# Outer products of key and value for eight decode samples: 8-row matmuls on TensorE, or ScalarE scaling value rows that a broadcast DMA has spread over the partitions

## The chip, the cores and the metric

One core of one Trainium2 chip runs the whole kernel as one launch. The metric is device time in microseconds (us). The kernel before takes 1415.7 us (median of 3 runs, 1415.12 to 1415.8). Engines go by the names of the profile: PE is TensorE (PEld its weight loads), ACT is ScalarE, DVE is VectorE, POOL is GpSimd, SP is SyncE. POOL and SP issue the DMAs; SPq is SP as the profile lists its DMA issues.

## The reference, cut to what matters

One step of a one-layer decoder: latent attention (MLA) and gated linear attention (GLA) are merged, then come cross attention over 256 memory tokens and a mixture of 32 experts (top 4). It runs for a prompt of 256 tokens and for 8 samples of one token each, all in float32. The change touches the recurrence of the samples alone. Each of the 8 samples has, for each of 4 heads, a state of 128 x 256 numbers:

```python
def gla_sample(q, k, v, la, state):
    def step(st, inp):
        qt, kt, vt, lat = inp
        st = jnp.exp(lat)[..., None] * st + kt[..., :, None] * vt[..., None, :]
        return st, jnp.einsum('bhd,bhdv->bhv', qt, st)
```

For sample b and head h the second term is the outer product of a key of 128 numbers and a value of 256. The new states are an output (512 KB per sample), and the query times the new state goes on into the layer.

## The kernel before, in words

Every engine has its own hand-written program; semaphores S("name") order them. Activations lie transposed, features on the partitions and the 264 tokens (256 of the prompt, 8 samples) along the row. Weights come in 2 MB pieces through ring slots of 16 KB per partition; SP issues them in the order of RING, each when the last reader of its slot is done (L439 to L445). Products go in a fixed order LIN through PSUM banks 0 to 3: `open_bank` waits until the product four places before it has been copied out. Transposes go in a fixed order TURN through banks 5 and 6. A transpose at an even place of TURN is copied out by DVE, at an odd place by ACT (`turn_out`), so taking one name out of TURN swaps the two engines for all names behind it: those of the GLA output (gt0 to gt3, L1012), the memory keys (xk, L1025), the cross attention (xp, xst) and the routing weights (cwt, L1246).

The stage around the change comes after the eight units of prompt attention (L900 to L917), from 218 to 257 us of the span:

- In unit 5, PE transposes the samples' keys (ks, L837), and DVE copies them out, 8 rows to a token. `k_rows` (L1975) are 8 copies of these rows in slot 3, in the copy of sample b all rows but row b set to zero. In unit 7, PE transposes the values: v0 to v3 of the prompt, then v4 and v5 of the samples (L838 to L844), the latter into `vs_tok`, 8 rows to a token.
- `outer_products(b)` on PE (L922): four matmuls with 8 rows of contraction, `k_rows` of b times `vs_tok`, give the four 128 x 256 outer products in banks 5 and 6. It waits until DVE is done with the products of sample b - 1 (state_new), and raises kv_sample.
- DVE (L2002 to L2010) waits for the old state of sample b (state_in) and for kv_sample, makes the new state in place with four `scalar_tensor_tensor`, and raises state_new.
- `state_times_q(b)` on PE (L933) multiplies the query by the new state and raises state_read.
- PE's loop (L952 to L960) is, for b = 0 to 7: outer_products(b); then product gg{b} of the output gate (b < 6) or the prompt's chunk scores A0, A1; then state_times_q(b - 1). After the loop comes state_times_q(7).
- ACT copies gg0 to gg5 out with Silu (L1524), waits for the eighth state_read (L1526), squares the samples' output, copies A0 and A1 out and turns out ko0 (L1527 to L1532). PE multiplies the prompt's keys and values next (L967 to L979).
- POOL (L592 to L602) has all state DMAs in one program. There are four state buffers in SBUF. For b = 0 to 7 it issues the load of state b; for b >= 4 it first waits until the store of state b - 4 has landed and until PE has read that state (L596, L597). For b >= 3 it then issues the store of state b - 3 (`store_state`, L551, which waits for state_new). At b = 2 it waits for the product uv7.
- SP loads the next use of slot 3 (weights zm0) when kv_sample is 8 (L441).

```python
            for b in range(8):
...
                if b >= 4:
                    pool.wait_ge(S(f"state_out{b % 4}"), 16)
                    pool.wait_ge(S("state_read"), b - 3)
                pool.dma_start(st_buf[b % 4], state_gla[0, b].rearrange("h k v -> k h v")).then_inc(S(f"state_in{b % 4}"), 16)
                if b >= 3:
                    store_state(b - 3)
```

Behind this stage stand the rest of GLA, the gates, the output products and the cross attention (to about 490 us), and then the experts, whose 384 MB of weights SP streams from about 418 us on (L475 to L494) as slots come free.

## Time and profile before

| | us |
|---|---|
| median of 3 runs (lowest, highest) | 1415.7 (1415.12, 1415.8) |
| the profiled execution's own time | 1419.78 |
| span of the profiled execution | 1418.0 |
| PE busy of the span | 1338.1 (94%) |
| DVE, ACT, POOL busy | 353.4, 252.4, 84.9 |
| granted TensorE clock, mean of the span | 0.992 |

The span is the stretch that the trace covers; the execution's own time has 1.8 us more around it. The profiled execution is 4.1 us longer than the median of the runs without a profile, so differences are made inside the trace and then put on the median. Busy time of an engine is not the same as work on the path that sets the end. The chain of waits follows that path back from the last instruction. A row of a timeline gives start, duration, engine, line, operation, output and inputs, and in brackets how long the engine had been idle before it and what ended that. Granted clock 1.00 is 2.4 GHz, 0.50 is 1.2 GHz.

### The profile page before, as it was taken

What the parts mean: (1) busy time and instruction counts of PE and PEld (TensorE: products, weight loads), DVE (VectorE), ACT (ScalarE), POOL (GpSimd) and SP (SyncE); (2) the same over time, 40 slices, a digit from 0 to 9 for tenths busy, and PEclk for the clock granted to TensorE, in tenths of its full rate; (3) what the DMA queues carried; (4) which work ended last, traced back from release to release, by engine and by line L of the source; (5) the groups of instructions that cost most, each with busy time, mean ns of one, the idle gap of its engine ahead of it and who ended that gap; (6) DMA issues with size and microseconds to landing.
All of it is one profiled execution on the core that took longest, in us unless ns stands there. A gap on an engine that the chain in (4) does not pass through costs nothing.

```text
span 1418.0 us, 17786 instructions
## 1 busy us (share of the span) xinstructions
PE 1338.1 (94%) x7300; PEld 710.4 (50%) x7300; DVE 353.4 (25%) x775; ACT 252.4 (18%) x543; POOL 84.9 (6%) x104
## 2 busy tenths in 40 slices
PE   7998999899999999999989989899999998998987
PEld 5746887588888734434433424334344243342433
DVE  2753343310134522212212202122022021220112
ACT  3323332421123501101101101011011010110102
POOL 1541211100101000000000000000000000000000
PEclk9999999999999999999999999999999999999999
DMA  9773555923647799999999999999999999999995
GB/s 332 240 262 125 193 181 161 326 98 140 247 169 273 285 428 427 428 428 429 429 428 428 429 428 428 429 428 428 420 429 429 429 428 428 429 428 427 429 427 224
DMA packets 62437, 494.75 MB, mean 349 GB/s; under 512 B 5247, under 2 KB 6472, under 8 KB 37816
## 3 DMA queue, kind: packets, MB, share of 16 engines
q1 hardware_dynamic: 50904, 453.95, 77.1%
q0 software_dynamic: 11488, 40.17, 8.4%
q8 instruction: 32, 0.52, 0.1%
q14 instruction: 13, 0.11, 0.0%
HBM read 487.05 MB, written 7.05 MB: 348 GB/s over the span
## 4 chain that ended last, share of the span: by engine, by line
PE 75%; DMA 20%; DVE 2%; issue 1%; ACT 0%; SPq 0%; POOL 0%; DVEq 0%
PE bank L1183 21%; PE bank L680 16%; PE bank L1210 13%; DMA ring<-in_w_gate_up 11%; DMA arena<-in_w_down 8%; PE bank L1222 4%; PE bank L1169 4%; PE bank L639 3%; PE bank L652 2%; PE bank L790 1%; PE bank L1190 1%; PE bank L704 1%; PE bank L1196 1%; PE bank L1119 1%; PE bank L1033 1%
## 5 line engine op out<-in xcount | busy, mean ns | idle before, releaser
L1183 PE MATMUL bank<-ring,arena 128*64 128x512 f32 x1536 | 344.9, 597 | 7.3 <-DMA ring<-in_w_gate_up 7.3
L1210 PE MATMUL bank<-arena 128*64 128x512 f32 x976 | 225.1, 613 | 32.0 <-DMA arena<-in_w_down 32.0
L1183 PEld LDWEIGHTS bank<-ring,arena 128*64 128x64 f32 x1536 | 104.1, 137 | 224.7 <-issue 205.9
L680 PE MATMUL bank<-arena,ring 128*128 128x264 f32 x896 | 204.9, 388 | 0.0
L680 PEld LDWEIGHTS bank<-arena,ring 128*128 128x128 f32 x896 | 168.2, 190 | 31.9 <-issue 3.9
L1210 PEld LDWEIGHTS bank<-arena 128*64 128x64 f32 x976 | 69.1, 140 | 174.1 <-issue 127.3
L2220 DVE TENSOR_TENSOR resid<-resid,bank 128x264 f32<-128x264 f32 x128 | 55.0, 429 | 375.5 <-PE bank L1222 374.0
L1183 PE MATMUL bank<-arena 128*64 128x512 f32 x512 | 115.5, 593 | 3.9 <-DMA arena<-in_w_gate_up 3.9
L2225 DVE TENSOR_SCALAR arena<-bank 128x512 f32<-128x512 f32 x32 | 22.0, 688 | 323.3 <-PE bank L1183 323.3
L1672 ACT COPY arena<-bank 64x512 f32<-64x512 f32 x63 | 36.5, 580 | 240.3 <-PE bank L1210 239.5
L1183 PEld LDWEIGHTS bank<-arena 128*64 128x64 f32 x512 | 36.3, 137 | 78.5 <-issue 66.8
L1351 ACT ACTIVATE arena<-bank 128x264 f32<-128x264 f32 (+6 forms) x120 | 46.8, 402 | 158.2 <-PE bank L680 117.0
L1664 ACT ACTIVATE arena<-arena 128x512 f32<-128x512 f32 x32 | 20.2, 630 | 306.0 <-DVE arena L2225 306.0
L1222 PE MATMUL bank<-arena 128*128 128x264 f32 x256 | 63.9, 392 | 0.0
L1660 ACT COPY arena<-bank 128x512 f32<-128x512 f32 x32 | 18.8, 587 | 243.5 <-PE bank L1196 243.4
L1169 PEld LDWEIGHTS bank<-arena 128*128 128x128 f32 x512 | 59.6, 192 | 1.0
L1169 PE MATMUL bank<-arena 128*128 128x128 f32 x512 | 60.0, 275 | 0.0
L1222 PEld LDWEIGHTS bank<-arena 128*128 128x128 f32 x256 | 45.9, 189 | 19.6 <-issue 13.0
L680 PE MATMUL bank<-ring 128*128 128x264 f32 (+1 forms) x192 | 44.4, 385 | 1.6 <-DVE ring L2061 1.4
L680 PEld LDWEIGHTS bank<-ring 128*128 128x128 f32 x192 | 35.7, 190 | 7.8 <-DVE ring L2061 1.8
L560 POOL DMA_INDIRECT ring<-in_cache_kv_latent,arena x32 | 33.6, 1050 | 95.9 <-PE bank L890 38.3
L1190 PE MATMUL bank<-arena 32*64 32x512 f32 x256 | 34.8, 612 | 1.5 <-DVE arena L2226 1.5
(317 smaller groups left out, 974.4 us busy)
## 6 DMA issues: line engine op xcount, KB each, us to landing
ring<-in_w_gate_up SPq DMA_DIRECT2D x96, 2048.0 KB, 29.6
arena<-in_w_down SPq DMA_DIRECT2D x61, 2048.0 KB, 22.7
arena<-in_w_gate_up SPq DMA_DIRECT2D x32, 2048.0 KB, 29.2
ring<-in_w_in SPq DMA_DIRECT2D x10, 2048.0 KB, 9.6
ring<-in_w_down SPq DMA_DIRECT2D x3, 2048.0 KB, 44.1
out<-arena POOLq DMA_DIRECT2D x10, 512.0 KB, 5.3
arena<-in_state_gla POOLq DMA_DIRECT2D x8, 512.0 KB, 4.8
ring<-in_w_o_mla SPq DMA_DIRECT2D x2, 2048.0 KB, 8.6
```

The source lines that it names most:

```text
L560: pool.indirect_dma_start(lat[j].rearrange("p a b -> p (a b)"), None, lat_rows, off).then_inc(S(f"lat{j}"), 16)
L639: mm = nc.tensor.matmul(lin_bank(name)[0:m, 0:width], l, r, start=(j == 0), stop=(j == len(parts) - 1))
L652: mm = nc.tensor.transpose(turn_bank(name)[0:m, at:at + k], src, ident[r:r + k, r:r + k])
L680: mm = nc.tensor.matmul(lin_bank(name)[0:m, 0:width], w(ring_name, nk, cols)[:, k, a:a + m], rhs[:, k, 0:width], start=(k == 0), stop=(k = ...
L1169: mm = nc.tensor.matmul(B[2 + 3 * half][:, P * k:P * k + P], hn_tok[:, tt, a:a + P], sel[:, tt, :], start=(tt == 0), stop=(tt == 1))
L1183: mm = nc.tensor.matmul(B[i // 2][CAP * (i % 2):CAP * (i % 2) + CAP, :], xg[:, k, CAP * e:CAP * e + CAP], slot(n)[:, a:a + 512], start=Fal ...
L1190: nc.tensor.matmul(B[q // 2][CAP * (q % 2):CAP * (q % 2) + CAP, :], pick_b[32 * q:32 * q + 32, e, :], b_gu[32 * q:32 * q + 32, :], start=T ...
L1210: mm = nc.tensor.matmul(B[4][CAP * half:CAP * half + CAP, :], hT[:, c, CAP * (k // 4):CAP * (k // 4) + CAP], slot(j)[:, a:a + 512], start= ...
L1222: nc.tensor.matmul(B[5 + c % 3][:, 0:T], y_rows[:, 128 * c:128 * c + 128], wselT, start=True, stop=True)\
L1351: nc.scalar.activation(dst, lin_bank(name)[0:m, 0:width] if src is None else src, func, **kw).then_inc(S("product_out"), 1)
L1672: nc.scalar.copy(y_rows[CAP * odd:CAP * odd + CAP, 512 * half:512 * half + 512], B[4][CAP * half:CAP * half + CAP, :])\
L2220: V.tensor_tensor(h_T[:, c, :], h_T[:, c, :], B[5 + c % 3][:, 0:T], ALU.add).then_inc(S("added"), 1)
```

## The change

PE makes no outer product any more, and the keys of the samples are not transposed (ks is gone from TURN). In unit 7, v4 and v5 are transposed ahead of v0 to v3. POOL writes the samples' value rows to a DRAM tensor `v_rows` (two DMAs of 16 KB), waits for them, and reads each sample's row of 4 KB back to all 128 partitions, 512 KB into one of four buffers `v_wide` in slot 3 (`widen_values`). The first two of these stand before its wait for uv7; for b = 2 to 7 one stands between the load of state b and the store of state b - 3, from b = 4 on behind a wait for kv_sample. They count on the semaphores lat0 to lat3. ACT then makes the outer product: four `activation(Copy)` of 128 x 256 from `v_wide` into banks 5 and 6, each scaled per partition by the key. ACT's order is gg0, outer 0, gg1, outer 1 to gg5, outer 5, outer 6, outer 7. PE's loop is gg0 to gg5, A0, A1, with state_times_q(b - 2) behind step b, and 6 and 7 after the loop. DVE loses the mask and the `k_rows`. ACT's copy of cwt is moved behind its first `gathered`. As ks is gone, DVE and ACT swap the transposes behind it.

```diff
@@ -112,7 +112,7 @@
 AT_UNIT = {1: ["pv0"], 2: ["pv1"], 3: ["ol0", "pv2"], 5: ["pv3"], 6: ["ol1"], 7: [f"uv{h}" for h in range(7)]}
 
 
-TURN_AT_UNIT = {1: ["P1_0", "P1_1"], 2: ["P1_2", "P1_3"], 5: ["ks"], 7: [f"v{n}" for n in range(6)]}
+TURN_AT_UNIT = {1: ["P1_0", "P1_1"], 2: ["P1_2", "P1_3"], 7: [f"v{n}" for n in (4, 5, 0, 1, 2, 3)]}
 
 
 LIN = (["cq0", "cq1", "ckv", "kr", "rotk", "mk0"]
@@ -329,15 +329,15 @@
         v_tok = xview(0, 2048, D)
         ko_tok = xview(2048, 1024, 512)
         AT = xview(3072, 512).rearrange("p (c h t) -> p c h t", c=2, h=H_GLA)
-        vs_tok, ks_tok, row_mask = view(A_SMALL + 256, 512), A[0:64, 14816:15072], view(15072, 32)
-        k_rows = slot(3)[0:64, 0:2048].rearrange("p (b n) -> p b n", b=SAMPLE)
+        vs_tok = view(A_SMALL + 256, 512)
+
+        v_wide = [slot(3)[:, 1024 * i:1024 * i + 1024] for i in range(4)]
+        v_rows = nc.dram_tensor("v_rows", (SAMPLE, H_GLA * DV), F32, kind="Internal").ap()
 
         def row_parts(name):
             if name[0] == "P":
                 c = int(name[3])
                 return [(past[:, 1, 512 * c:512 * c + 512], P, (0, 512))]
-            if name == "ks":
-                return [(ks_tok[32 * g:32 * g + SAMPLE, :], SAMPLE, (256 * g, 256 * g + 256)) for g in range(2)]
             n = int(name[1])
             c, g = n // 2, n % 2
             if n < 4:
@@ -589,13 +589,27 @@
                     pool.dma_start(o_memv_p[0, 0].rearrange("(t p) h d -> p t (h d)", p=P), memv).then_inc(S("stored"), 16)
 
             pool.wait_ge(S("gla_qk"), 1)
+            def widen_values(b):
+                if b >= 4:
+                    pool.wait_ge(S("kv_sample"), b - 3)
+                pool.dma_start(v_wide[b % 4], v_rows[b:b + 1, :].to_broadcast([P, H_GLA * DV])).then_inc(S(f"lat{b % 4}"), 16)
+
             for b in range(8):
                 if b == 2:
+                    turned(pool, "v4")
+                    turned(pool, "v5")
+                    for g in range(2):
+                        pool.dma_start(v_rows[:, 512 * g:512 * g + 512], vs_tok[32 * g:32 * g + SAMPLE, :]).then_inc(S("v_rows"), 16)
+                    pool.wait_ge(S("v_rows"), 32)
+                    widen_values(0)
+                    widen_values(1)
                     lin_full(pool, "uv7")
                 if b >= 4:
                     pool.wait_ge(S(f"state_out{b % 4}"), 16)
                     pool.wait_ge(S("state_read"), b - 3)
                 pool.dma_start(st_buf[b % 4], state_gla[0, b].rearrange("h k v -> k h v")).then_inc(S(f"state_in{b % 4}"), 16)
+                if b >= 2:
+                    widen_values(b)
                 if b >= 3:
                     store_state(b - 3)
             for b in range(5, 8):
@@ -832,16 +846,13 @@
                     pe.wait_ge(S("past_exp"), 2)
                     for c in (2 * u - 2, 2 * u - 1):
                         turn(f"P1_{c}", [(128 * t, past[:, 1, 512 * c + 128 * t:512 * c + 128 * t + 128]) for t in range(4)])
-                if u == 5:
-                    lin_done(pe, "gk3")
-                    turn("ks", [(128 * h, gkT[:, h, PROMPT:T]) for h in range(H_GLA)])
                 if u == 7:
                     lin_done(pe, "gv7")
+                    for g in range(2):
+                        turn(f"v{4 + g}", [(128 * j, gvT[:, 4 * g + j, PROMPT:T]) for j in range(4)])
                     for tt in range(2):
                         for g in range(2):
                             turn(f"v{2 * tt + g}", [(128 * j, gvT[:, 4 * g + j, P * tt:P * tt + P]) for j in range(4)])
-                    for g in range(2):
-                        turn(f"v{4 + g}", [(128 * j, gvT[:, 4 * g + j, PROMPT:T]) for j in range(4)])
 
             def values_up(h):
                 w_ready(pe, "uv")
@@ -915,20 +926,8 @@
                 unit_values(u)
             lin_done(pe, "att7")
             values_up(7)
-            turned(pe, "ks")
-            turned(pe, "v4")
-            turned(pe, "v5")
-
-            def outer_products(b):
-
-                if b:
-                    pe.wait_ge(S("state_new"), b)
-                pe.wait_ge(S("k_rows"), b + 1)
-                for h in (0, 2, 1, 3):
-                    rows, i = slice(32 * (h // 2), 32 * (h // 2) + SAMPLE), h % 2
-                    mm = nc.tensor.matmul(B[5 + h // 2][:, DV * i:DV * i + DV], k_rows[rows, b, 128 * i:128 * i + 128],
-                                          vs_tok[rows, DV * i:DV * i + DV], start=True, stop=True)
-                mm.then_inc(S("kv_sample"), 1)
+            turned(pe, "v2")
+            turned(pe, "v3")
 
             def state_times_q(b):
                 pe.wait_ge(S("state_new"), b + 1)
@@ -950,13 +949,13 @@
 
             pe.wait_ge(S("q_wide"), 1)
             for b in range(8):
-                outer_products(b)
                 if b < 6:
                     project([f"gg{b}"], f"gg{b // 4}", 8, 512, n_T, first=128 * (b % 4))
                 else:
                     chunk_scores(b - 6)
-                if b >= 1:
-                    state_times_q(b - 1)
+                if b >= 2:
+                    state_times_q(b - 2)
+            state_times_q(6)
             state_times_q(7)
 
             pe.wait_ge(S("gla_kout"), 1)
@@ -1521,8 +1520,25 @@
                             src=lin_bank(name)[:, 0:32].rearrange("p (j h) -> p h j", j=4))
                 out(f"att{h}", big2[:, h, 0:PROMPT], width=PROMPT)
             out("uv7", big3[:, 7, :])
+            def outer_products(b):
+
+                act.wait_ge(S(f"lat{b % 4}"), 16 * (8 + b // 4 + 1))
+                if b:
+                    act.wait_ge(S("state_new"), b)
+                else:
+
+                    turned(act, "v2")
+                    turned(act, "v3")
+                for h in range(H_GLA):
+                    ins = nc.scalar.activation(B[5 + h // 2][:, DV * (h % 2):DV * (h % 2) + DV], v_wide[b % 4][:, DV * h:DV * h + DV], ACT.Copy,
+                                               scale=gkT[:, h, PROMPT + b:PROMPT + b + 1])
+                ins.then_inc(S("kv_sample"), 1)
+
             for b in range(6):
                 out(f"gg{b}", silu_gg[:, b, :], ACT.Silu)
+                outer_products(b)
+            outer_products(6)
+            outer_products(7)
             act.wait_ge(S("state_read"), 8)
             nc.scalar.activation(gla_junk[:, 0:DV], SCORE_BANK[:, 0:DV], ACT.Square, accum_out=gla_sum[:, 8:9]).then_inc(S("o_sample_squared"), 1)
             for tt in range(2):
@@ -1639,9 +1655,6 @@
             act.wait_ge(S("top_shifted"), 1)
             nc.scalar.activation(weights, weights, ACT.Exp).then_inc(S("top_exp"), 1)
             order[0] += 1
-            if TI["cwt"] % 2:
-                turn_out("cwt", [(wselT[0:NE, :], NE, (0, T))])
-
             def gathered(g):
                 for half in range(2):
                     act.wait_ge(S("gathered"), 2 * g + half + 1)
@@ -1690,6 +1703,8 @@
 
             def experts(p):
                 gathered(p * (NE // 2))
+                if isinstance(p, int) and TI["cwt"] % 2:
+                    turn_out("cwt", [(wselT[0:NE, :], NE, (0, T))])
                 expert_pair(0, p, True)
                 with act.Fori(1, NE // 2 - 1) as q:
                     expert_pair(q, p, False)
@@ -1966,13 +1981,6 @@
                     V.tensor_tensor(gtmp[:, :, pr], gtmp[:, :, pr], gkT[:, :, pr], ALU.mult).then_inc(S("gla_kout"), 1)
                 if u == 11:
                     V.tensor_tensor(gkT[:, :, pr], gkT[:, :, pr], gb[:, :, pr], ALU.mult).then_inc(S("gla_qk"), 1)
-                if u == 10:
-                    V.memset(ks_tok, 0.0)
-                    link(V.tensor_reduce(row_mask, ident.rearrange("p (j e) -> p e j", j=4), AX, ALU.add))
-                if u in (12, 13):
-                    turned(dve, "ks")
-                    for b in range(4 * u - 48, 4 * u - 44):
-                        V.tensor_scalar(k_rows[:, b, :], ks_tok, row_mask[0:64, b:b + 1], None, ALU.mult).then_inc(S("k_rows"), 1)
                 if u == 15:
                     link(V.memset(q_wide, 0.0))
                     V.tensor_copy(q_wide.rearrange("p h b k -> p h (b k)")[:, :, 0:256:33], gqT[:, :, PROMPT:T]).then_inc(S("q_wide"), 1)
```

## Rows read from the trace of the kernel before

**Rows 1.** part 2 of the page: DMA busy tenths in 40 slices of 35.45 us each.
```profile
DMA  9773555923647799999999999999999999999995
```

**Rows 2.** waits of PE, 500 us to the end: us in total, times, longest.
```profile
PE bank L1210 <- DMA arena<-in_w_down: 32.0, 16, 4.0
```

**Rows 3.** chain in order of time, 197 to 247 us: start us, us, what.
```profile
197.56 0.44 PE bank L652 x4
...
218.51 1.06 PE bank L929 x8
219.58 3.76 PE bank L680 x16
...
228.16 0.57 PE bank L936 x8
```

**Rows 4.** the same chain, 251 to 282 us.
```profile
251.48 1.67 DVE arena L2008 x4
...
256.15 0.68 PE bank L936 x8
...
259.77 1.16 PE bank L975 x8
...
281.54 14.44 PE bank L680 x64
```

**Rows 5.** timeline of PE, the 8-row products of the last sample.
```profile
253.19 1.14 PE L929 MATMUL bank<-arena,ring 8*128 8x256 f32 x8 [0.64 <-DVE arena L2008]
```

**Rows 6.** timeline of POOL: L598 loads states, L553 stores them.
```profile
221.66 0.76 POOL L553 DMA_DIRECT2D out<-arena  x1 [1.35 <-DVE arena L2008]
229.32 0.75 POOL L598 DMA_DIRECT2D arena<-in_state_gla  x1 [6.90 <-PE bank L936]
...
235.63 0.75 POOL L598 DMA_DIRECT2D arena<-in_state_gla  x1 [4.81 <-DMA out<-arena]
...
241.75 0.75 POOL L598 DMA_DIRECT2D arena<-in_state_gla  x1 [4.62 <-DMA out<-arena]
...
248.34 0.76 POOL L598 DMA_DIRECT2D arena<-in_state_gla  x1 [5.09 <-DMA out<-arena]
```

**Rows 7.** DMA issues at 221 to 223 us, one store: KB, us to landing.
```profile
out<-arena POOLq DMA_DIRECT2D x1, 512.0 KB, 4.3
```

**Rows 8.** DMA issues at 236.3 to 237.2 us, load and store behind it.
```profile
arena<-in_state_gla POOLq DMA_DIRECT2D x1, 512.0 KB, 4.6
out<-arena POOLq DMA_DIRECT2D x1, 512.0 KB, 5.1
```

**Rows 9.** busy us of each engine, clock, DMA share, GB/s, 237 to 241 us.
```profile
237.00:241.00 4.00, 4.00 (x27) 2.63 (x26) 0.30 (x1) 0.39 (x1) 0.13 (x1) 1.00 0.88 262
```

**Rows 10.** the same columns where the last DMA is a broadcast row.
```profile
1397.00:1398.00 1.00, 1.00 (x7) 0.34 (x6) 0.00 (x0) 0.00 (x0) 0.00 (x0) 1.00 0.88 360
```

**Rows 11.** timeline of DVE: copy of a v transpose; four new-state instructions.
```profile
210.76 0.69 DVE L1737 COPY ring<-bank 128x512 f32<-128x512 f32 x1 [0.75 <-PE bank L652]
...
246.09 1.66 DVE L2008 SCALAR_TENSOR_TENSOR arena<-arena,bank 128x256 f32<-128x256 f32 x4 [3.74 <-PE bank L929]
```

**Rows 12.** ACT by shape: 128x256 with a scale from SBUF; mean ns.
```profile
L1535 ACT ACTIVATE ring<-bank,arena 128x256 f32<-128x256 f32 x1 | 0.5, 474 | 0.0
```

**Rows 13.** timeline: two such ACT copies, and the gt transposes.
```profile
297.34 0.66 PE L652 MATMUL bank<-consts_sb,arena 128*128 128x128 f32 x4 [0.50 <-ACT arena L1564]
...
298.04 0.84 ACT L1564 ACTIVATE arena<-bank,gains_t 128x256 f32<-128x256 f32 x2 [0.75 <-PE bank L652]
...
298.86 0.66 PE L652 MATMUL bank<-consts_sb,arena 128*128 128x128 f32 x4 [0.86 <-DVE arena L2048]
```

**Rows 14.** timeline of PE and windows around its idle stretch of 3.67 us.
```profile
112.04 8.45 PE L790 MATMUL bank<-arena,ring 32*32 32x512 f32 x192 [3.67 <-DVE arena L1841]
...
112.00:113.00 1.00, 0.96 (x30) 0.45 (x33) 0.00 (x0) 0.00 (x0) 0.83 (x1) 0.52 0.91 303
...
115.00:116.00 1.00, 1.00 (x48) 0.49 (x32) 0.00 (x0) 0.00 (x0) 0.00 (x0) 0.78 0.94 373
```

## The prediction

> **What bounds the kernel now.** I read the page's row of DMA shares first: the DMA engines are full from the 15th of the 40 slices to the 39th, some 62% of the span [rows 1], and in that stretch PE waits for weights 32 us in sixteen pieces [rows 2]. The experts are a stream of weights that starts when the trunk frees its slots, and PE is just behind it. So a shift of the trunk's end moves the end of the kernel by as much. The chain in order of time then shows what sets the trunk around the change: PE alone, an 8-row product of 1.06 us, gg of 3.76, state times query of 0.57, again and again [rows 3], up to the last sample, where PE waits 0.64 us for DVE's states [rows 4, 5]. PE looks like the bound. The timeline of POOL shows a second chain under it that the chain of waits does not name. From 229.32 us on, each state load leaves POOL when a store has landed, and the next store stands right behind that load in the same queue: loads at 229.32, 235.63, 241.75 and 248.34, the last three released by a store [rows 6]. I call this the ladder. Its step is 6.12 us at the least disturbed place; load 7 lands 4.6 us after its issue [rows 8], at 252.9, and the last outer product is ready at 254.33 [rows 5]. The ladder is 1.4 us short of being the bound.
>
> **PE's part.** Gone are eight products of 1.06 us (8.5 us) and the transpose of ks, 0.44 us [rows 3]. Moving v4 and v5 ahead of v0 to v3 keeps their number and the copy-out that paces them; I cost it at nothing. So gg0 starts 1.06 + 0.44 us earlier, at 219.58 - 1.5 = 218.1 [rows 3], and is full at 221.8. It waits now for v2 and v3, which are the last turned out in place of v4 and v5: no new time. The steps of PE are then 3.76, from gg2 on 3.76 + 0.57 = 4.33: gg2 and query 0 end at 229.9, gg5 is full at 242.4.
>
> **ACT's part.** No row has an ACT copy from SBUF to a bank. The nearest one, from a bank to SBUF with a scale per partition, takes 0.474 us [rows 12], and two in a row take 0.84, so each further one adds 0.37 [rows 13]. Four take 0.47 + 3 x 0.37 = 1.58 us. Bounds: nothing excludes half of it, 0.8; 2.4 if the direction costs half again. The Trainium skill (ScalarE: Activation LUTs, step-by-step, clean up before approximating) says that ScalarE writes to PSUM with less delay than to SBUF; it would make the outer product shorter, and no row here shows by how much. DVE's four instructions stay at 1.66 [rows 11]. Banks 5 and 6 are not doubled, so ACT waits for DVE and DVE for ACT: a sample takes 1.58 + 1.66 + 0.1 of handovers = 3.34 us, less than PE's 4.33 and hidden by it until gg5. Copy and Silu share a table in the trace (no table load between gg5 and the copies behind it), so none is added.
>
> **The values' way through DRAM.** v4 and v5 are now the first two of the six. The second of the six is copied out by 210.76 + 0.69 = 211.5 in the trace [rows 11]. Two issues on POOL at 0.75 each at most, landing at most like a store thirty times as large, 4.3 us [rows 7]: the rows are in DRAM by 217.3, and widening 0, taking a load's 4.6, lands by 221.9 [rows 8]. ACT needs it at 221.88 + 0.39 = 222.3. Hidden, with little cover at the bound; behind it stand widening 1, the wait for uv7 and loads 2 and 3 with their widenings, 4 x 0.75 us from 217.8 on, all issued by 222.
>
> **The ladder's part decides.** State 0 is new at 221.84 + 0.39 + 1.58 + 1.66 + 0.1 = 225.6. POOL issues its store 0.3 later, it lands 4.3 later [rows 7], and load 4 leaves 0.3 after that: 230.5, against 229.32 before. It also waits for query 0, done at 229.9. Now each step has load, widening, store in one queue. Before, the store landed 5.1 us after its own issue behind one load, against 4.3 alone [rows 7, 8], and the two moved 262 GB/s x 4 us = 1.05 MB [rows 9]. What a third transfer of 512 KB adds: at least nothing, if it fills gaps between the others; at the rate of a broadcast row, the last DMA before the output, whose slice ran at 360 GB/s and 0.88 share, that is 409 when full [rows 10], 1.28 us; at twice that, 2.5, if 128 reads of one row of 4 KB get in each other's way. I take 1.25. The POOL issue of 0.75 lies inside. So the step is 6.12 + 1.25 = 7.37, and load 7 leaves at 230.5 + 3 x 7.37 = 252.6. ACT needs widening 7, which stands behind the load as the store did: 0.75 + 5.1 later, at 258.45. Then 1.58 + 1.66 + 0.15: state 7 is new at 261.85. Before it was new when the last product's end, 254.33, 0.1 of handover and 1.66 of DVE were over: 256.1, just ahead of query 7 at 256.15 [rows 4, 5, 11]. That is **5.7 us later**. PE's saving of 9 us is spent waiting, since behind A1 it has nothing but the queries.
>
> Bounds of this term: a step of 6.12 and widening 7 landing as the load, 4.6 after its issue, give 248.9 + 0.75 + 4.6 + 3.4 = 257.6, that is +1.5; a step of 8.6 gives load 7 at 256.4, widening 7 at 263.5, +10.8.
>
> **The clock.** PE will idle twice, between queries 5, 6 and 7, some 6.8 us each (a step less 0.6). The trace has an idle stretch of 3.67 us behind which the granted clock is 0.52 and comes back in the fourth us of work (0.78) [rows 14]: 1.2 GHz for some 3.5 us. Here query 7 costs 0.6 more, and the keys' and values' products after it, 1.16 and more [rows 4], run some 3.5 us at half speed, of which half is lost: 1.8. Sum 2.4 us, bounds 0 and 3.6 (the whole stretch lost). The Trainium skill (TensorE: Matmul & The Clock Gate, HAM oscillation) describes such gaps behind which each burst starts cold; the trace agrees with it at the one place named.
>
> **The swapped transposes.** gt0 and gt2 go from ACT to DVE, gt1 and gt3 the other way. DVE now waits for ACT's gt0 before it serves gt1; PE pays 0.50 + 0.86 us [rows 13]. With DVE first and ACT beside it, some 0.5 is left: -0.8 (bounds 0 and -1.3). xk, xp and cwt I cost at nothing: PE's products and the sigmoid's wait cover them; if that cover is gone, a copy of 0.7 shows. DVE's k_rows were not on the chain of waits, so their end gives nothing. zm0 is loaded when kv_sample is 8, 5.7 us later than before; it is needed at 281.5 before [rows 4], 27 us behind its issue, and that moves with it.
>
> **Sum:** 5.7 + 2.4 - 0.8 = +7.3 us. The profiled execution took 1419.8, so 1427.1 for its like; on the median, 4.1 below it, **1423.0**.
>
> **Rivals.** *The widening is free:* step 6.12. For it: the queue is at 0.88 share in the busy stretch and idle between. The sum is +1.5 + 2.4 - 0.8 = +3.1, 1418.8; without the clock term +0.7, 1416.4. The Trainium skill (DMA: Bandwidth & Descriptors, anatomy of one DMA) gives 2.0 us and the bytes at 436 GB/s for a DMA from GpSimd; its estimate for three of 512 KB is 5.6 us, a step of 5.9, and so this rival. The same rule gives 3.2 us for one state load, where the row has 4.6 [rows 8], so I trust the increment only.
>
> *The broadcast is slow:* step 8.6, +10.8 + 2.4 - 0.8 = +12.4, 1428.1. For it: no POOL broadcast of 512 KB is in the trace, and all engines read one row at once. Against: [rows 10].
>
> *The ladder does not bind, and the change is faster:* the place is POOL's wait for the store before a load. If loads left it with steps under 4.4 us, load 7 would be out by 243.7 and ACT and DVE would set the end: gg5 at 242.4, 0.4, then three samples at 3.34: state 7 at 252.8, -3.3, no long idle, -0.8: -4.1, 1411.6. For it: PE carries the chain of waits there. Against: a store alone takes 4.3 and 0.3 to be noticed, and the steps of before never were below 6.1 [rows 6].
>
> **How the numbers follow.** A measurement of this kernel can tell about 0.2%, 2.8 us, from no change. Forecast 0.50, slow broadcast 0.15, free widening with the clock term 0.15, without it 0.08, no ladder 0.12. Faster is the last, 0.12. Same is 0.08 and half of the 0.15 that sits at the edge (1418.8 against 1418.5): 0.15. Slower is the rest, 0.73. The range leaves out the faster case and the far end of the slow one: 1416 to 1430; the forecast's own is 1420 to 1426.
>
> **What would show it.** Right: POOL's loads 5 to 7 about 7.4 us apart; ACT's outer products 6 and 7 released by a DMA into the ring; PE idle some 6 us before queries 6 and 7 and at clock 0.5 behind; state 7 about 5.7 us later; expert stage as long as before. Wrong: outer products released by DVE or PE, no idle stretch on PE over 2 us, ladder steps near 6.1 or below, or ACT's four copies far from 1.6 us. A time under 1416 makes the ladder wrong as the deciding step.

## The result, and the profile after

| | before | after |
|---|---|---|
| median of 6 runs each, us | 1415.14 (1412.92 to 1415.8) | 1421.16 (1420.53 to 1421.78) |
| profiled execution, its span, us | 1419.78, 1418.0 | 1421.78, 1419.9 |
| granted clock of TensorE over the span | 0.992 | 0.981 |

The ratio is 1.0041, 95% interval 1.0031 to 1.0051: the change makes the kernel slower by 6.0 us (4.4 to 7.2). The forecast was 1423.0, and 1420 to 1426 as its own range. The two spans differ by 1.9 us only. That is the trace of before: its execution lay 4.1 us over its median. The stages show where. I cut both traces at the same marks, starts or ends of rows (that of uv7 lies 0.07 us ahead of the end of its row, in all traces alike): the end of TensorE's product uv7, DVE's end of new state 0 and of new state 7, the first kv product, the start of zm, SyncE's first issue of an expert's gate and up weights, the end.

| stage, us | before | after | second run of after |
|---|---|---|---|
| start to end of uv7 | 218.45 | 214.14 | 213.70 |
| uv7 to new state 0 | 2.92 | 7.38 | 7.38 |
| uv7 to new state 7 | 37.65 | 45.13 | 45.24 |
| state 7 to the first kv product | 3.67 | 4.07 | 4.07 |
| first kv product to zm | 21.70 | 22.67 | 22.00 |
| zm to the first expert's issue | 136.31 | 135.27 | 135.27 |
| from there to the end | 1000.2 | 998.6 | 999.8 |

Of the 4.3 us ahead of uv7 the change explains 0.75: the transpose of ks, 0.44, and 0.31 at the turns of the values (timeline of PE, before and then after). Waiting for copies, TensorE idles 0.88 us there in before, and 0.33 with v4 and v5 first; from the first of these transposes to the product behind them it is 4.13 us in the two traces without the change (before, e3) and 3.82 or 3.83 in the eleven with it.

```profile
212.94 0.60 PE L652 MATMUL bank<-consts_sb,arena 128*8 128x128 f32 x4 [0.35 <-DVE ring L1737]
```

```profile
208.06 1.17 PE L666 MATMUL bank<-consts_sb,arena 128*128 128x128 f32 x8 [0.16 <-DVE ring L1752]
```

The rest, 3.6 us, arose between 62 and 112 us, in code that the change does not touch. Of the thirteen profiled executions in this document (all but c0's), five ended uv7 at 213.7 to 214.8 us and eight at 217.2 to 219.4. This goes with the chip: the four on the chip whose before has a median of 1415.7 are all early, the seven on the two chips with 1419.96 and 1420.59 all late, with the change or without it. Of the first two traces the chips are not known; after's is early and before's late, which would fit a profile of before on another chip than its times, but that is not shown. So the 3.6 us are left out of what follows. What remains of the change is -0.75 ahead of uv7, +7.48 up to state 7, +0.40 and +0.97 behind it, -1.04 behind zm: +7.1 us (+6.5 in the second run of after), beside the measured 6.0.

**The ladder.** Timeline of POOL in the kernel after (start us, busy us, engine, line; L610 loads a state, L595 widens a value row, L553 stores a state); it answers [rows 6]:

```profile
212.63 1.08 POOL L595 DMA_DIRECT2D ring<-v_rows  x2 [3.81 <-DMA v_rows<-arena]
...
226.69 0.76 POOL L610 DMA_DIRECT2D arena<-in_state_gla  x1 [4.11 <-DMA out<-arena]
...
234.42 0.75 POOL L610 DMA_DIRECT2D arena<-in_state_gla  x1 [5.67 <-PE bank L935]
235.16 0.55 POOL L595 DMA_DIRECT2D ring<-v_rows  x1
235.70 0.76 POOL L553 DMA_DIRECT2D out<-arena  x1
242.25 0.76 POOL L610 DMA_DIRECT2D arena<-in_state_gla  x1 [5.79 <-DMA out<-arena]
...
249.92 0.75 POOL L610 DMA_DIRECT2D arena<-in_state_gla  x1 [5.62 <-DMA out<-arena]
```

Each rung is load, widening, store, and then the wait for that store. The steps are 7.73, 7.83 and 7.67 us, where before had 6.31, 6.12 and 6.59. (The second load is put down to PE's query, which had ended at 229.8; POOL waited for two things, and the store was the late one.) The DMA issues of 241 to 248 us (KB, median us from issue to landing) answer [rows 8]: the load lands as before, the store behind two others takes 6.1 in place of 5.1.

```profile
arena<-in_state_gla POOLq DMA_DIRECT2D x1, 512.0 KB, 4.5
ring<-v_rows POOLq DMA_DIRECT2D x1, 512.0 KB, 5.3
out<-arena POOLq DMA_DIRECT2D x1, 512.0 KB, 6.1
```

**Who waits for it.** ScalarE's outer products 5 to 7 (timeline of ACT) each end an idle stretch that a widening ends, and four copies take 1.67 us:

```profile
240.44 1.67 ACT L1533 ACTIVATE bank<-ring,arena 128x256 f32<-128x256 f32 x4 [2.15 <-DMA ring<-v_rows]
248.36 1.67 ACT L1533 ACTIVATE bank<-ring,arena 128x256 f32<-128x256 f32 x4 [6.25 <-DMA ring<-v_rows]
255.84 1.67 ACT L1533 ACTIVATE bank<-ring,arena 128x256 f32<-128x256 f32 x4 [5.81 <-DMA ring<-v_rows]
```

The chain in order of time (start us, us, what), which in before ran on PE here [rows 3, 4], now runs through the store of state 3, for which load 7 waits, and the widening of value row 7:

```profile
243.54 6.09 DMA out<-arena
...
249.92 0.74 POOL arena L610
250.66 5.15 DMA ring<-v_rows
...
255.84 1.68 ACT bank L1533 x4
...
257.61 1.67 DVE arena L2016 x4
...
259.32 1.13 PE bank L935 x8
```

**TensorE idles, and its clock falls.** Timeline of PE; the same eight products of a query, 0.64 us while the clock is up, take 1.08. [Rows 5] were the busy counterpart:

```profile
243.93 1.08 PE L935 MATMUL bank<-arena 128*32 128x256 f32 x8 [3.69 <-DVE arena L2016]
251.85 1.08 PE L935 MATMUL bank<-arena 128*32 128x256 f32 x8 [6.84 <-DVE arena L2016]
259.32 1.08 PE L935 MATMUL bank<-arena 128*32 128x256 f32 x8 [6.39 <-DVE arena L2016]
...
263.34 4.53 PE L974 MATMUL bank<-ring 64*128 64x256 f32 x24 [1.03 <-DVE ring L1752]
```

In windows of 1 us (busy us of PE, its weight loads, DVE, ACT, POOL; then granted clock, DMA share, GB/s) the clock goes down to 0.50, which is 1.2 GHz, inside the idle stretch of 3.69 us, and comes back after PE has been busy from 263.34 on, as it did in [rows 14]:

```profile
242.00:243.00 1.00, 0.00 (x0) 0.00 (x0) 0.79 (x2) 0.11 (x1) 0.75 (x1) 0.88 0.00 0
243.00:244.00 1.00, 0.07 (x4) 0.08 (x8) 0.87 (x3) 0.00 (x0) 1.00 (x3) 0.50 0.62 61
...
266.00:267.00 1.00, 1.00 (x8) 0.64 (x6) 0.38 (x1) 0.59 (x2) 0.00 (x0) 0.67 1.03 401
267.00:268.00 1.00, 1.00 (x9) 0.67 (x7) 0.93 (x3) 0.96 (x2) 0.00 (x0) 1.00 1.06 410
```

**Behind zm.** The gt transposes, which answer [rows 13]: eight in one go, one idle stretch of 0.53 us in place of 0.50 and 0.86.

```profile
300.35 1.04 PE L666 MATMUL bank<-consts_sb,arena 128*128 128x128 f32 x8
...
301.92 1.09 PE L666 MATMUL bank<-consts_sb,arena 128*128 128x128 f32 x8 [0.53 <-DVE arena L2056]
```

The expert stage is as before: the DMA row of the page is full again from the 15th slice on [rows 1], and PE's waits for down weights are 31.0 us in sixteen pieces [rows 2].

```profile
DMA  9783467924646799999999999999999999999995
```

```profile
PE bank L1209 <- DMA arena<-in_w_down: 31.0, 16, 4.0
```

### The profile page after: what moved, and what is told of

The parts are those of the page before. It is cut to its first block, busy times and chain, and to the rows that moved or that the text cites. A ratio compares the mean times of both kernels' runs of the same rounds, so it can differ in the third digit from the quotient of the medians.

```text
span 1419.9 us, 17679 instructions
## 1 busy us (share of the span) xinstructions
PE 1331.4 (94%) x7232; PEld 709.2 (50%) x7232; DVE 350.1 (25%) x763; ACT 266.3 (19%) x575; POOL 89.3 (6%) x114
## 4 chain that ended last, share of the span: by engine, by line
PE 73%; DMA 22%; DVE 2%; POOL 1%; issue 1%; ACT 1%; SPq 0%; DVEq 0%
PE bank L1182 21%; PE bank L694 16%; PE bank L1209 13%; DMA ring<-in_w_gate_up 11%; DMA arena<-in_w_down 8%; PE bank L1221 4%; PE bank L1168 4%; PE bank L653 2%; PE bank L666 2%; PE bank L1189 1%; PE bank L718 1%; DMA ring<-in_cache_kv_latent,arena 1%; PE bank L1195 1%; PE bank L1118 1%; PE bank L1032 1%; DMA out<-arena 1%
```

## The experiments

They ran on three chips, whose before had medians of 1419.96 us (c0, e1, e2, e3), 1415.7 (a1, e4, e5, e6) and 1420.59 (e7, e8, e9, e10), so only ratios are set beside each other. This table has what all were read for. "Trunk" is the sum of the stages from uv7 to the first expert's issue against before's, less 0.75 where ks is gone and the values are turned in the new order: what the time ought to move by, by the trace. The last column is the measured ratio to before, with its interval; the quotient of the two medians differs from it by up to 0.0011 (0.9984 for e6).

| kernel | steps between loads 4 to 7, us | uv7 to state 7 | state 7 to zm | trunk, us | ratio, 95% |
|---|---|---|---|---|---|
| before | 6.31, 6.12, 6.59 | 37.65 | 25.37 | 0 | 1 |
| after | 7.73, 7.83, 7.67 | 45.13 | 26.74 | +7.1 | 1.0041 (1.0031, 1.0051) |
| a1, after again | 7.66, 8.07, 7.79 | 45.24 | 26.07 | +6.5 | 1.0034 (1.0021, 1.0047) |
| e1, four widenings | 6.29, 6.40, 6.40 | 37.58 | 26.06 | -1.2 | 1.0008 (0.9998, 1.0018) |
| e2, early stores | 4.25, 5.75, 3.83 | 37.94 | 27.72 | +0.9 | 0.9998 (0.9988, 1.0008) |
| e3, before with early stores | 5.39, 5.39, 5.40 | 37.65 | 26.61 | +1.2 | 0.9998 (0.9988, 1.0007) |
| e4, half widenings | 6.71, 6.79, 6.65 | 41.30 | 26.74 | +3.2 | 1.0021 (1.0012, 1.0030) |
| e5, widenings on SyncE | 8.16, 6.17, 6.54 | 39.91 | 27.36 | +2.5 | 1.0015 (1.0004, 1.0027) |
| e6, spread out | 2.55, 6.56, 4.28 | 33.98 | 27.29 | -3.5 | 0.9973 (0.9961, 0.9984) |
| e7, kept busy | 7.72, 7.98, 7.77 | 45.39 | 25.34 | +5.9 | 1.0035 (1.0022, 1.0047) |
| e10, store first | 6.49, 6.40, 6.67 | 44.24 | 27.47 | +6.9 | 1.0034 (1.0023, 1.0044) |
| e8, parity back | 7.76, 7.88, 7.72 | 45.56 | 27.86 | +9.7 | 1.0053 (1.0037, 1.0070) |
| e9, spread out and busy | 2.75, 5.59, 4.12 | 32.94 | 25.35 | -6.5 | 0.9958 (0.9944, 0.9973) |

The measured ratios follow the trunk within some 2.5 us; a profile is one execution, and the stage from the first expert's issue to the end, the same code in all, took 998.6 to 1001.3. The times moved less than was expected of them: by their ratios e1, e2, e5 and e6 lie some 4, 6, 3 and 9 us under after, where 8, 12, 7 to 8 and 14 had been expected. The stages below show where.

**Before again (c0).** The kernel before, unchanged.

> The kernel before, unchanged, for a second trace of it. Between 62 and 112 us the first trace of before lost some 3.7 us against the trace of after in a part that the change does not touch (keys gathered and turned). If that is chance, this trace has state 7 new near 252 us of the span and a span near 1414; if it belongs to the kernel before, state 7 is new at 256 again and the span is 1418.

One execution, of 1735.03 us at a mean granted clock of 0.752. Its stages can't be set beside the others', and those of before rest on the one trace; e3, which moves only stores in it, has the same 37.65 us up to state 7.

**Four widenings (e1).** The wait of outer products 4 to 7 is put on the first widening of the buffer, so that no new one is needed.

```
-                if b >= 2:
+                if b in (2, 3):
                     widen_values(b)
...
-                act.wait_ge(S(f"lat{b % 4}"), 16 * (8 + b // 4 + 1))
+                act.wait_ge(S(f"lat{b % 4}"), 16 * 9)
```

> After without the widenings of samples 4 to 7 (their outer products use the value rows of samples 0 to 3, so the states and outputs of four samples differ). Ladder theory: the steps between state loads go back from 7.7 to 6.1 us, load 7 leaves 5 us earlier and ACT has no landing of a widening behind it; state 7 is new at 251.4 in place of 259.3, time about 1413 (-8). Rival, the handover of ACT and DVE over two banks sets the end: nothing changes, 1421. Rival, the later start of load 4 sets it: at most 1 us, 1420.

With nothing between load and store the steps are 6.3 to 6.4, and state 7 comes 7.5 us earlier than in after, where the theory had 7.9: the whole loss up to state 7 is due to the four widenings. It has two parts. Load 7 leaves 4.5 us earlier than in after; the other 3.0 us lie behind it, where state 7 hangs on the landing of load 7 and no longer on that of the widening behind it, with ScalarE's copies. Timeline of POOL, then two lines of DVE's, which now waits for states and not for outer products:

```profile
235.72 0.75 POOL L610 DMA_DIRECT2D arena<-in_state_gla  x1 [4.78 <-DMA out<-arena]
236.46 0.76 POOL L553 DMA_DIRECT2D out<-arena  x1
242.12 0.76 POOL L610 DMA_DIRECT2D arena<-in_state_gla  x1 [4.90 <-DMA out<-arena]
```

```profile
246.97 1.66 DVE L2016 SCALAR_TENSOR_TENSOR arena<-arena,bank 128x256 f32<-128x256 f32 x4 [2.27 <-DMA arena<-in_state_gla]
253.16 1.66 DVE L2016 SCALAR_TENSOR_TENSOR arena<-arena,bank 128x256 f32<-128x256 f32 x4 [4.53 <-DMA arena<-in_state_gla]
```

The time, 1419.79, is before's and not under it; the trunk had -1.2 us, as the stage behind state 7 lost 0.7 here too. State 7 comes 37.58 us after uv7, and in before 37.65: with every new widening gone from the ladder, TensorE's 8.5 us of 8-row products removed buy nothing up to state 7. That is the second half of the answer: they are worth nothing up to state 7 as long as a rung takes 6.3 us.

**Early stores (e2, e3).** Store b - 3 goes ahead of the wait for load b, in after (e2) and in before (e3).

```
                 if b >= 4:
+                    store_state(b - 3)
                     pool.wait_ge(S(f"state_out{b % 4}"), 16)
                     pool.wait_ge(S("state_read"), b - 3)
...
-                if b >= 3:
-                    store_state(b - 3)
+                if b == 3:
+                    store_state(0)
```

> After with POOL's stores of states 1 to 4 issued ahead of the wait for the store before, not behind the next load; nothing else. Ladder theory: loads 5 to 7 leave by the buffer's own cycle, load 7 near 238.6 instead of 249.9; ACT and DVE then set the end with three samples behind gg5 at 3.4 us each, state 7 at 248.4 instead of 259.3, PE idles under 3 us at a time, the clock stays up: 1409 (-12), below before. Rival, handover of ACT and DVE: 1421. Rival, the bytes themselves (three transfers per sample at the DMA engines' rate): steps near 4.5 us, 1416 to 1418.

> The same reordering of stores in the kernel before. Ladder theory: the ladder was 1.4 us short of being its bound, PE's products set the end, so the time stays within 1 us of 1415. If the reordering alone is worth something whatever makes the products: -5 us or more, like the gain in after.

In before it breaks the ladder and the time stays (e3): its loads leave every 5.4 us, released by the query, as PE was the chain there. In after (e2) it loosens the ladder too (loads 6 and 7 are still released by a store, but sooner), and state 7 comes 7.2 us earlier, not the 10.9 expected. What is late next is the widening: number 6 left at 241.74 and was there at 249.23, 7.5 us later. Timeline of ACT:

```profile
249.23 1.67 ACT L1534 ACTIVATE bank<-ring,arena 128x256 f32<-128x256 f32 x4 [4.21 <-DMA ring<-v_rows]
253.53 1.67 ACT L1534 ACTIVATE bank<-ring,arena 128x256 f32<-128x256 f32 x4 [2.64 <-DMA ring<-v_rows]
```

A sample moves 1.5 MB here instead of 1 MB, and from 234 to 250 us the DMA engines are at 0.92 to 0.99 share and 310 to 353 GB/s, where after has 0.53 to 0.68 and 153 to 241. With most of the waits gone their rate is the next limit. This tells the ladder (waits in a row) from the bytes: both are there, the ladder first.

**After again (a1)** repeats the kernel after on the second chip.

> After, unchanged, for its time against before on this chip and a second trace. Ladder theory: steps between state loads of 7.7 us as in its first trace, state 7 new 45.1 us behind the end of uv7, from there to the start of zm 26.7; the time is 5 to 7 us above before on the same chip (ratio 1.004).

1421.88 us, and the same ladder; what differs from the first trace of after is the stage from kv to zm (22.00 against 22.67).

**Half widenings (e4).** From sample 4 on the widening carries half of the row; the other half of the buffer keeps the values of four samples before.

```
-                pool.dma_start(v_wide[b % 4], v_rows[b:b + 1, :].to_broadcast([P, H_GLA * DV])).then_inc(S(f"lat{b % 4}"), 16)
+                n = H_GLA * DV if b < 4 else 512
+                pool.dma_start(v_wide[b % 4][:, 0:n], v_rows[b:b + 1, 0:n].to_broadcast([P, n])).then_inc(S(f"lat{b % 4}"), 16)
```

> After with the widenings of samples 4 to 7 cut to 256 KB each (heads 0 and 1; heads 2 and 3 of these samples use the value rows of the sample four before, so states and outputs differ). If the bytes queued ahead of the store set the step, it lies half way between 6.35 us (no widening, seen before) and 7.74: 7.0 to 7.1, and state 7 is new 42.5 us behind uv7; time 2.5 us under after. If the step is paid per DMA (its issue, its completion), it stays at 7.7 and state 7 at 45: the time of after.

Steps of 6.65 to 6.79, state 7 at 41.30 where 42.5 was expected. With no third transfer the step is 6.36 (e1's mean), with 256 KB 6.72, with 512 KB 7.74 (after's mean): the first half costs 0.36 and the second 1.0. So the price is not the issue alone (0.55 us, and the same in e4 and after), and it grows faster than the bytes: the stores of these rungs land in 4.95 to 5.13 us in e4 and in 5.99 to 6.15 in after.

**Widenings on SyncE (e5).** The same eight, on SyncE's queue, released only by v_rows and by the buffer; zm's weights, which that queue loads next, then wait behind them. POOL issues none and waits for none, and ScalarE waits on the semaphores of the new issues.

```
                 if name == "zm0":
+                    sp.wait_ge(S("v_rows"), 32)
+                    for b in range(8):
+                        if b >= 4:
+                            sp.wait_ge(S("kv_sample"), b - 3)
+                        sp.dma_start(v_wide[b % 4], v_rows[b:b + 1, :].to_broadcast([P, H_GLA * DV])).then_inc(S(WIDE[b % 4]), 16)
                     sp.wait_ge(S("kv_sample"), 8)
...
-                if b >= 2:
-                    widen_values(b)
...
-                act.wait_ge(S(f"lat{b % 4}"), 16 * (8 + b // 4 + 1))
+                act.wait_ge(S(WIDE[b % 4]), 16 * (b // 4 + 2))
```

> After with all eight widenings issued by SP (its own queue, before its wait ahead of zm0), each as soon as v_wide is free; POOL's order of loads and stores is untouched. If the place in POOL's queue is what costs, the steps go back to 6.1 to 6.4 us, ACT's outer products never wait for a widening, state 7 is new 37 us behind uv7 and the time is 7 to 8 us under after, 1 to 2 under before. If it is the shared DMA engines whatever the queue, the steps stay above 7.2 and the time within 3 us of after.

The last widening leaves at 231.4, outer products 6 and 7 wait for a state and not for one, and the last two steps are 6.17 and 6.54, as without widenings. The step from load 4 to load 5 is 8.16 while the last of them move (timeline of POOL):

```profile
227.22 0.75 POOL L613 DMA_DIRECT2D arena<-in_state_gla  x1 [4.43 <-DMA out<-arena]
...
235.38 0.75 POOL L613 DMA_DIRECT2D arena<-in_state_gla  x1 [6.66 <-DMA out<-arena]
...
241.55 0.75 POOL L613 DMA_DIRECT2D arena<-in_state_gla  x1 [4.67 <-DMA out<-arena]
```

State 7 is at 39.91, 5.2 us ahead of after's and 2.9 behind the 37 I expected. A second queue does not hide the bytes: the store issued at 227.97 us, beside widenings of the other queue, landed in 7.1 us, that of the same rung in after in 6.15. What it gives is that the widenings are done before the last rungs.

**Store first (e10).** One exchange in after's queue: load b, store b - 3, then widening b.

```
-                if b >= 2:
+                if b in (2, 3):
                     widen_values(b)
                 if b >= 3:
                     store_state(b - 3)
+                if b >= 4:
+                    widen_values(b)
```

> After, with one pair of transfers exchanged on POOL's queue from sample 4 on: load b, store b-3, and only then widening b (after: load b, widening b, store b-3). The same bytes, the same queue, one more thing ahead of nothing. Theory of the prediction (the ladder is load b waits for the landing of store b-4, and the widening stands ahead of that store in the queue): the steps between loads fall from 7.7 to 6.2 to 6.5 us as in before, state 7 comes at 41 to 42 us after the end of uv7 instead of 45.2, and the time is 3 to 4 us under after, about that of before. Rival (only the bytes count, the engines of the queue share themselves among what is outstanding): the store shares the transfer time with the widening issued behind it, the steps stay at 7.2 us or more, state 7 at 43.5 to 45, and the time is at most 1.5 us under after. A widening issued later may now be waited for by ScalarE: then DVE's new states wait for kv products and no longer for loads, which would show in the same step.

Neither theory had it whole. The steps are back at 6.49, 6.40 and 6.67 with every byte still moved: the ladder is a matter of what stands ahead of the store, and the rival's 7.2 is out. But state 7 gains 0.9 us only, inside the rival's 43.5 to 45, as the widening is late now. The chain of e10:

```profile
245.34 5.64 DMA out<-arena
...
251.26 0.75 POOL arena L610
252.02 0.74 POOL out L553
252.76 7.45 DMA ring<-v_rows
...
260.23 1.68 ACT bank L1535 x4
```

In after the last widening took 5.15 us from its issue, here, behind a load and a store, 7.45. Load 7 leaves 31.84 us after uv7 instead of 35.78, 3.9 earlier; the widening lands 9.0 after it instead of 5.9, and 3.1 are given back. (The widenings of 5 and 6 took 6.6 and 6.3 from issue to use; behind that of 7 a further store was issued, at 253.48.) What stands last in a rung is late; after made the store late, e10 the operand.

**Spread out (e6).** This takes the findings together: a widening leaves as soon as its buffer is free, ahead of the store; a store goes ahead of the wait for the next load; ScalarE makes the outer product ahead of its copy of gg out of the bank; TensorE queries state b - 1 beside gg b.

```
-                if b >= 4:
-                    pool.wait_ge(S(f"state_out{b % 4}"), 16)
-                    pool.wait_ge(S("state_read"), b - 3)
...
-                if b >= 2:
+                if b < 4:
+                    load_state(b)
+                if b in (2, 3):
                     widen_values(b)
-                if b >= 3:
-                    store_state(b - 3)
-            for b in range(5, 8):
-                store_state(b)
+            for s in range(8):
+                if s < 4:
+                    widen_values(s + 4)
+                store_state(s)
+                if 1 <= s < 5:
+                    pool.wait_ge(S(f"state_out{(s + 3) % 4}"), 16)
+                    pool.wait_ge(S("state_read"), s)
+                    load_state(s + 3)
...
-                if b >= 2:
-                    state_times_q(b - 2)
-            state_times_q(6)
+                if b >= 1:
+                    state_times_q(b - 1)
...
-                out(f"gg{b}", silu_gg[:, b, :], ACT.Silu)
                 outer_products(b)
+                out(f"gg{b}", silu_gg[:, b, :], ACT.Silu)
```

> A version that should beat both: widening 4 to 7 issued as soon as its buffer is free and ahead of the store, each store before the wait for the one before it, ACT makes outer product b before it copies gg b, PE multiplies by the query one step earlier. Theory: with no ladder the samples run at ACT plus DVE, 3.4 us each; load 7 leaves 24 us behind uv7, state 7 is new at 31 (45.1 in after, 37.6 in before), PE idles under 3 us at a time; time 14 us under after and 8 under before. Rival, the DMA engines' rate (1.5 MB per sample): state 7 at 36 to 38, the time of before less the 1 us of the gt transposes.

1413.38 us, ratio 0.9973: faster than both kernels. State 7 is at 33.98 where 31 was expected; of the outer products only the first waits for a widening (2.26 us), but DVE waits for states 4, 5 and 6. Which of the four reorderings is worth how much was not taken apart; the early stores alone (e2) gave 37.94. One of DVE's three waits (its timeline):

```profile
243.38 1.66 DVE L2020 SCALAR_TENSOR_TENSOR arena<-arena,bank 128x256 f32<-128x256 f32 x4 [3.19 <-DMA arena<-in_state_gla]
```

**Kept busy (e7).** Throwaway transposes on TensorE in the idle stretches of after.

```
             def state_times_q(b):
+                for _ in range({5: 26, 6: 56, 7: 52}.get(b, 0)):
+                    nc.tensor.transpose(B[4][:, 0:P], ident, ident)
                 pe.wait_ge(S("state_new"), b + 1)
```

> After, with throwaway 128x128 transposes of the constant identity put on TensorE where it waits for new states 5, 6 and 7 (26, 56 and 52 of them; one takes about 0.109 us at the full clock, so they fill some 2.8, 6.1 and 5.7 us of idles of 3.69, 6.84 and 6.39 us). Nothing of the result hangs on them. Theory (the fall of the granted clock to 0.50 over 243 to 266 us stretches the work after the last state): the clock stays at 1.00, the queries take 0.64 us instead of 1.08, from state 7 to the first kv product 3.7 us instead of 4.07, from there to the start of zm 21.7 instead of 22.0 to 22.7, and the kernel gets 0.7 to 1.4 us faster than after; the loads of states keep their steps of 7.7 us, state 7 stays at 45.2 us after the end of uv7. Rival: the ladder is what it is, and the stretch behind state 7 (26.1 to 26.7 us in after, 25.4 in before) is not the clock's; then the clock is high and the stretch stays, and the time is that of after. The prediction's 2.4 us for the clock would be seen if the stretch fell to 24.3.

Timeline of PE: the transposes, and query 7 at 0.64 us.

```profile
257.93 5.90 PE L934 MATMUL bank<-consts_sb 128*128 128x128 f32 x52
264.88 0.64 PE L937 MATMUL bank<-arena 128*32 128x256 f32 x8 [1.05 <-DVE arena L2018]
...
268.44 2.00 PE L976 MATMUL bank<-ring 64*128 64x256 f32 x16 [1.90 <-DVE ring L1754]
270.90 1.13 PE L976 MATMUL bank<-ring 64*128 64x256 f32 x8 [0.46 <-ACT arena L1352]
```

The clock is 1.00 in every window from 235 to 279 us, and state 7 to zm takes 25.34 us, before's 25.37, instead of 26.74 and 26.07. So what after loses there is the clock, and it is 1.4 and 0.7 us in its two traces, where the clock stays at 0.50 for 7.4 and 3.6 us behind state 7. It can be more: in e10, with the same work behind state 7 and on the chip of e7, it stays there for 9.0 us, and the stretch takes 27.47, 2.1 more than in e7 (e2: 9.5 us and 27.72). The row of e10 in which it comes back:

```profile
272.00:273.00 1.00, 1.00 (x7) 0.49 (x5) 0.72 (x3) 0.69 (x2) 0.00 (x0) 0.69 1.06 414
```

The two lines of L976 show why: at full speed the kv products wait 1.90 and 0.46 us for the copies of DVE and ScalarE, so that a slower TensorE loses only part of its stretch. The time, ratio 1.0035, can't tell 1 us from nothing; the stages can. The steps of the ladder stay, as they should.

**Parity back (e8).** A throwaway entry between ko1 and gt0.

```
-        + ["ko0", "ko1"] + [f"gt{h}" for h in range(4)]
+        + ["ko0", "ko1", "dm"] + [f"gt{h}" for h in range(4)]
...
+            turn("dm", [(0, ident[0:8, 0:8])])
             turned(pe, "ko0")
             turned(pe, "ko1")
...
+            turn_out("dm", [(vs_tok[0:8, 0:8], 8, (0, 8))])
             for h in range(4):
                 lin_done(dve, f"kv{2 * h + 1}")
```

> After, with one throwaway entry in the list of turns between ko1 and gt0: an 8x8 transpose, copied out by VectorE to a place nobody reads any more. It turns the parity of every later entry back, so that gt0 to gt3, xk, xp and cwt go to the engines that they had in before. Theory (the removed turn ks exchanged the engines of the gt turns, and that gave 1.0 us): from the start of zm to the first issue of an expert's gate and up weights 136.3 us as in before, instead of 135.27, and all ahead of zm as in after: the time 1.0 us above after. Rival (the 1.0 us came of something else that the change does, such as the ks work gone or the times at which the queue is free): the stretch stays at 135.27 us.

The stretch is 136.31 again, and the idles are before's (timeline of PE):

```profile
308.30 0.66 PE L666 MATMUL bank<-consts_sb,arena 128*128 128x128 f32 x4 [0.49 <-ACT arena L1581]
309.81 0.66 PE L666 MATMUL bank<-consts_sb,arena 128*128 128x128 f32 x4 [0.86 <-DVE arena L2058]
```

So the 1.04 us are the exchange of the two engines at gt, which came to this change by chance with the removal of one turn. The time of e8 lies further above after's than 1 us (1.0053); its profiled execution had the clock low until 274 us, and its interval is wide.

**Spread out and kept busy (e9).** e6 with 28 and 18 such transposes ahead of queries 6 and 7.

```
             def state_times_q(b):
+                for _ in range({6: 28, 7: 18}.get(b, 0)):
+                    nc.tensor.transpose(B[4][:, 0:P], ident, ident)
                 pe.wait_ge(S("state_new"), b + 1)
```

> The version of e6 (each widening from 4 on issued as soon as its buffer is free and ahead of the stores, each store ahead of the wait for the next load, ScalarE's products ahead of its eviction of gg, the query a step earlier), and with it throwaway transposes on TensorE ahead of queries 6 and 7 (28 and 18 of them, some 3.1 and 2.0 us of idles of 3.59 and 2.44 us). Theory: the clock stays high behind the last state, state 7 to kv 3.7 us instead of 4.07, kv to zm 21.7 instead of 23.2, 1 to 1.9 us faster than e6 (which was 0.9973 of before). Rival: the stretch from kv to zm is bound by the landing of store 7 (5 to 6 us) or by loads of weights that waited for the ladder, then it stays at 23 us whatever the clock.

1414.27 us where before is 1420.59: ratio 0.9958 (0.9944 to 0.9973), the best of all. State 7 to zm is 25.35 instead of 27.29; the rival, a bound by store 7 or by weights, is out. Its interval and e6's overlap, so that it is faster than e6 rests on the stages.

```profile
251.10 0.64 PE L942 MATMUL bank<-arena 128*32 128x256 f32 x8 [0.25 <-DVE arena L2022]
```

## Why the prediction was right, and where its terms were off

**The deciding step held.** The forecast was that POOL's ladder becomes the bound, that a widening between load and store stretches each step, that ScalarE waits for it and TensorE's saved 9 us are spent idle. The trace after shows each of these, and e1, e4 and e10 show that it is the widening ahead of the store. Counted from the end of uv7 (the prediction had it at 218.0, the trace at 214.14): load 4 was put at 12.5 us and left at 12.55; state 0 at 7.6 and new at 7.38; widening 7 landing 5.85 after load 7 and 5.9 in the trace. The values' way through DRAM was hidden as forecast: v_rows left at 207.76, widening 0 at 212.63, and outer product 0 waited for gg0.

**The step was mis-sized.** 7.37 predicted, 7.74 measured in the mean. Of these 0.37 us, 0.22 are the start: I took before's least disturbed step, 6.12, and its three have a mean of 6.34. The other 0.15 are the third transfer, priced at 1.25, which adds 1.40 to that mean. The sentence at fault there is "The POOL issue of 0.75 lies inside". It does not: the rung is the load's 0.75, the widening's 0.55, the store's landing of 6.1 and 0.3 to 0.6 until POOL goes on; before it was 0.75, 5.1 to 5.3, and the same 0.3 to 0.6. So the third transfer costs some 0.9 of landing and 0.55 of issue. Three steps make 1.1 us, ScalarE's four copies 1.67 for 1.58 another 0.1: state 7 came at 45.13 after uv7 instead of the 43.85 predicted. The Trainium skill (DMA: Bandwidth & Descriptors, Anatomy of one DMA) gives, as an estimate, 1.2 us for 512 KB more at its 436 GB/s. The store's landing grew by 0.9 here, a little under that, and the issue came on top.

**The clock term was over-sized for these traces.** 2.4 predicted, 1.4 and 0.7 in the two traces of after, and all of it gone in e7; e10 and e2, at 2.1 and 2.4, come up to it. The place was right (two idle stretches of 6.84 and 6.39 us, query 7 at 1.08, clock 0.50 behind it); the clock had already fallen in a shorter one, of 3.69 us, ahead of query 5. The step that failed is "run some 3.5 us at half speed, of which half is lost". The low stretch is 3.6 us in one trace and 7.4 in the other, and a fifth of it is lost, not half: the products wait for the copies of DVE and ScalarE between them, so part of the loss was slack. The Trainium skill (TensorE: Matmul & The Clock Gate, HAM oscillation) holds that bursts behind such gaps start cold; after agrees, with query 7 at 1.08 us, and without the long gaps e7 has it at 0.64.

**The swapped transposes** gave 1.04 for the 0.8 predicted, shown by e8. Of the costs put at nothing, the order of the v turns was worth -0.31 us, by fewer waits for copies; xk and xp left no mark, as the whole 1.04 us are there when gt is done (17.97 us from the start of zm in before, 16.93 in after). Whether cwt did can't be told within the spread of the expert stage.

**So the sum** of 7.3 us met a measured 6.0, with one term 1.3 too small (7.04 for 5.7), one 1.0 to 1.7 too large, and 0.55 more saved than forecast at gt and at the v turns: that the sum agrees so well is luck in part, as the errors cancel. Trunk sums of the traces (6.5, 7.1) lie in the upper part of the measured interval; what the missing 0.5 to 1.1 us are stays open, as the expert stage moves by 2.7 us between executions of the same code. The rivals: the free widening falls with e1 (it costs 1.4 a step), the slow broadcast falls as well (a widening lands in 5.3, the step is 7.74 and not 8.6). The faster case named a mechanism that exists, loads that leave without a long wait for the store, and e2 and e6 show it: with most of these waits out of the way state 7 comes 7 to 11 us earlier than in after. As a forecast it failed, since after has the waits.

## What to carry to other kernels

Before replacing work of the engine on which the chain of waits runs, look for a second chain just under it: here loads that wait for the landing of a store, 1.4 us from being the bound, made 9 us saved on TensorE worthless, and the new operand's transfer, placed inside its rung, made it a loss. In one queue a rung costs what is issued between its load and its store, and the landing of what is ahead; issue a transfer as soon as its buffer is free and not beside the one that it resembles in the code (e6, with ScalarE's and TensorE's order changed beside it: 11 us earlier with the same bytes). Where TensorE is left idle for microseconds, throwaway products can keep its clock up: 134 transposes in e7 and 46 in e9 held it at 1.00 throughout this stage, and in e7 the steps of the ladder stayed.

## What was not expected of the hardware

- The last of three queued transfers of 512 KB pays, whichever it is: the store 6.1 us (after), the widening 6.3 to 7.45 (e10, chain above), against 5.1 to 5.6 for the second and 4.3 to 5.1 for the first in the two. Half of the bytes in the middle costs 0.36 us a step, all of them 1.4.
- 128 reads of one row of 4 KB are no slower than other transfers of 512 KB here: in after, widenings land 4.4 to 8.6 us after issue, median 5.3, and loads of states 4.3 to 8.1, median 4.6, and POOL spends 0.55 us on the issue against 0.75 for a state.
- The clock can fall without a long idle stretch. In e3 TensorE idled 0.64 us twice, as in before, and the granted clock still went down (windows of 2 us), while before's execution kept 3.67 and 21.70 us behind state 7. What made it fall there stays open, and one trace is not enough to lay such a fall on a change.

```profile
254.00:256.00 2.00, 1.61 (x28) 0.73 (x26) 1.46 (x4) 0.00 (x0) 0.28 (x1) 1.00 0.61 193
256.00:258.00 2.00, 1.75 (x12) 1.01 (x13) 0.39 (x3) 0.74 (x4) 0.65 (x1) 0.61 0.95 244
258.00:260.00 2.00, 1.12 (x6) 0.71 (x4) 1.77 (x4) 1.97 (x4) 0.10 (x1) 0.50 1.05 341
```

- ScalarE copies 128x256 from SBUF to a bank with a scale per partition at 1.66 us for four, 0.1 more than the estimate from copies the other way.
